# A feed-forward stage with split matmuls: one of its four input sums is made by GpSimd

## The reference

```python
h = rmsnorm(x, pre_ffn_norm[l])
f = (jax.nn.silu(h @ ffn_w_gate[l]) * (h @ ffn_w_up[l])) @ ffn_w_down[l]
x = x + rmsnorm(f, post_ffn_norm[l])
```

## Time and profile before

| | |
|---|---|
| median of 3 runs | 2581.53 us (2581.36 to 2581.83) |
| the profiled execution's own time | 2586.55 us |
| its span, first to last instruction | 2584.8 us |
| mean granted TensorE clock | 0.984 |
| TensorE busy | 2440.1 us (94%) |
| VectorE busy | 1441.7 us (56%) |
| ScalarE busy | 1065.3 us (41%) |
| GpSimd busy | 356.4 us (14%) |

### The profile page before, as it was taken

The page is one execution under the profiler, slowest core; times in us unless marked ns, Lnnn a source line. Parts: engine busy times, 40 slices in busy tenths (PEclk is TensorE's granted clock), DMA queues, the critical chain, the costliest instruction groups (busy, mean ns, idle before and its releaser), DMA issues. The chain is left out here.

```text
span 2584.8 us, 34173 instructions
## 1 busy us (share of the span) xinstructions
PE 2440.1 (94%) x12048; PEld 2028.8 (78%) x12048; DVE 1441.7 (56%) x1990; ACT 1065.3 (41%) x1877; POOL 356.4 (14%) x369
## 2 busy tenths in 40 slices
PE   7999999999899999999999898888899999999997
PEld 6788888877688888787878788887777788888886
DVE  3656566665423232364541477775468777776556
ACT  4767677776312121242222343432333323223444
POOL 0323333333000000000000235352000000000000
PEclk9999999999899999999999999999999999999999
DMA  3112111111212121332233210100333444337764
GB/s 129 34 33 67 34 59 41 50 33 33 87 46 80 48 81 49 114 106 72 89 113 115 90 50 25 49 24 0 122 111 122 171 159 170 139 142 251 246 187 171
DMA packets 98113, 241.74 MB, mean 94 GB/s; under 512 B 8800, under 2 KB 34784, under 8 KB 96608
## 3 DMA queue, kind: packets, MB, share of 16 engines
q1 hardware_dynamic: 98016, 240.50, 27.7%
HBM read 177.29 MB, written 63.18 MB: 93 GB/s over the span
## 5 line engine op out<-in xcount | busy, mean ns | idle before, releaser
L52 PE MATMUL psG<-h_hi,w_hi 128*128 128x512 f32 x1408 | 350.8, 399 | 15.0 <-ACT w_hi L77 6.5
L82 DVE TENSOR_TENSOR w_lo<-w_raw,w_hi 128x1024 fp32r<-128x1024 f32 x102 | 129.3, 1269 | 420.2 <-ACT w_hi L77 419.8
L52 PE MATMUL psG<-h_hi,w_lo 128*128 128x512 f32 x1408 | 339.8, 390 | 0.0
L52 PE MATMUL psG<-h_lo,w_hi 128*128 128x512 f32 x1408 | 339.6, 390 | 0.0
L52 PEld LDWEIGHTS psG<-h_hi,w_hi 128*128 128x128 f32 x1408 | 269.9, 193 | 73.9 <-issue 12.6
L52 PEld LDWEIGHTS psG<-h_lo,w_hi 128*128 128x128 f32 x1408 | 263.7, 188 | 54.8
L52 PEld LDWEIGHTS psG<-h_hi,w_lo 128*128 128x128 f32 x1408 | 263.5, 188 | 54.7
L77 ACT CAST w_hi<-w_raw 128x1024 fp32r<-128x1024 f32 x104 | 109.1, 1050 | 355.7 <-PE psG L52 317.2
L366 POOL TENSOR_TENSOR sb_later_lo<-sb_later,sb_later_hi 128x512 fp32r<-128x512 f32 (+3 forms) x80 | 90.6, 1133 | 173.7 <-ACT sb_later_hi L395 173.7
L1430 POOL MEMSET m_k_prev<- 128x128 f32 x1 | 0.2, 204 | 802.0 <-POOLq L1141 802.0
L530 DVE SCALAR_TENSOR_TENSOR sb_sp<-psA,sb_tmp 128x128 f32<-128x128 f32 (+2 forms) x96 | 53.5, 557 | 73.3 <-ACT sb_tmp L384 70.8
(11 more groups left out here) (471 smaller groups left out, 5243.2 us busy)
## 6 DMA issues: line engine op xcount, KB each, us to landing
w_raw<-in_units SPq DMA_DIRECT2D x140, 512.0 KB, 3.7
w_raw<-hidden_blocks SPq DMA_DIRECT2D x77, 256.0 KB, 2.9
features<-p_res SPq DMA_DIRECT2D x24, 512.0 KB, 2.8
w_spare<-in_units SPq DMA_DIRECT2D x22, 512.0 KB, 4.3
hidden_blocks<-features_T SPq DMA_DIRECT2D x11, 1024.0 KB, 3.9
down_sums<-w_spare SPq DMA_DIRECT2D x22, 512.0 KB, 3.4
ff_raw_up<-down_sums SPq DMA_DIRECT2D x44, 256.0 KB, 3.2
m_feat<-features SPq DMA_DIRECT2D x7, 1536.0 KB, 7.5
```

Of the source, the lines that this page charges most:

```text
L52: return pe.matmul(out, lhs, rhs, start=first, stop=last, skip_group_check=True)
L82: dve.tensor_tensor(self.lo[c % 2][:] if dest is None else dest, self.raw[c % 2][:], hi.bitcast(F32), ALU.subtract).then_inc(self.lo_done, 1)
```

## The change

The sum t2 is made by GpSimd's three instructions, in a program of its own for this block, in a tile `t3_raw` of 128x2048. That tile lies where t2's low part will be: `t_lo[:, 2]`, so `split_t(2)` writes its result over its own input. GpSimd's first sum waits for nothing, the others each for the one before, by the new semaphore `t3_made`; ScalarE's `turned(2)` waits for its third step. VectorE's three sums for t2 go. The other three sums stay with VectorE, t1 stays in `X2`, and the second sum for t3 gets a wait for the first. The values waited for on `turned_done` become smaller by what is gone (TensorE's 12 and 14 become 9 and 11, ScalarE's 11 becomes 9). To make room for the new semaphore, `spilled` and `stored` become one, `stored`, and the last wait of SyncE counts both kinds.

```diff
+            t3_raw = nc.alloc_sbuf_tensor_at("ff_t3_raw", [P, 4, HALF], F32, offset=nc.sbuf_base - 2 * 16 * HALF)
...
+        t_raw = [T_X[0], T_X[1], t3_raw[:], T_X[0]]
...
-                    sp.wait_ge(stored, 16 * NT)
+                    sp.wait_ge(stored, 32 * PAIRS + 16 * NT)
...
+            @block.gpsimd
+            def _(pool):
+                hq = lambda t, r, c: t[:, 4 * r:4 * r + 4, c * HALF:(c + 1) * HALF].bitcast(F32)
+                for n, (a, b, op) in enumerate(((hq(hT_hi, 1, 1), hq(hT_hi, 0, 1), ALU.subtract), (t3_raw[:], hq(hT_lo, 1, 1), ALU.add),
+                                                (t3_raw[:], hq(hT_lo, 0, 1), ALU.subtract))):
+                    if n:
+                        pool.wait_ge(t3_made, n)
+                    pool.tensor_tensor(t3_raw[:], a, b, op).then_inc(t3_made, 1)
...
                     elif q >= 3:
                         act.wait_ge(plain, 4)
-                        act.wait_ge(turned_done, 11)
+                        act.wait_ge(turned_done, 9)
...
                 def turned(n, need):
-                    act.wait_ge(turned_done, need)
-                    act.copy(t_hi[:, n], T_X[0 if n in (0, 3) else 1]).then_inc(t_hi_done, 1)
+                    act.wait_ge(t3_made if n == 2 else turned_done, need)
+                    act.copy(t_hi[:, n], t_raw[n]).then_inc(t_hi_done, 1)
...
-                    turned(2, 11)
+                    turned(2, 3)
...
                 def split_t(n):
                     dve.wait_ge(t_hi_done, n + 1)
-                    TT(t_lo[:, n], T_X[0 if n in (0, 3) else 1], t_hi[:, n].bitcast(F32), ALU.subtract).then_inc(turned_done, 1)
+                    TT(t_lo[:, n], t_raw[n], t_hi[:, n].bitcast(F32), ALU.subtract).then_inc(turned_done, 1)
...
                     TT(X1, hq(hT_hi, 1, 0), X2, ALU.subtract).then_inc(turned_done, 1)
-                    dve.wait_ge(turned_done, 8)
-                    TT(X2, hq(hT_hi, 1, 1), hq(hT_hi, 0, 1), ALU.subtract).then_inc(turned_done, 1)
+                    split_t(2)
                     dve.wait_ge(turned_done, 9)
-                    TT(X2, X2, hq(hT_lo, 1, 1), ALU.add).then_inc(turned_done, 1)
-                    dve.wait_ge(turned_done, 10)
-                    TT(X2, X2, hq(hT_lo, 0, 1), ALU.subtract).then_inc(turned_done, 1)
-                    split_t(2)
-                    dve.wait_ge(turned_done, 12)
                     for s in (sum3, sum1, sum2):
                         s(0, 1, 0)
```

More of the change, by code:

```diff
@@ L1986, in ring_raw @@
             return W.raw[r // 2][:, cols], raw_up[:, r // 2, cols]
-        plain, turned_done, t_hi_done = (sem(n) for n in ("plain", "turned_done", "t_hi_done"))
+        plain, turned_done, t_hi_done, t3_made = (sem(n) for n in ("plain", "turned_done", "t_hi_done", "t3_made"))
         raw_here = [sem(f"raw_here{s}") for s in range(2)]
@@ L1992, in layer2_ffn @@
         p1_done, evac, silu_done, mul = (sem(n) for n in ("p1_done", "evac", "silu_done", "mul"))
-        own_done, spilled, dw_sum, dw_stored = (sem(n) for n in ("own_done", "spilled", "dw_sum", "dw_stored"))
+        own_done, stored, dw_sum, dw_stored = (sem(n) for n in ("own_done", "stored", "dw_sum", "dw_stored"))
         r_here = [sem(f"r_here{s}") for s in range(R)]
@@ L1996, in layer2_ffn @@
         p1_b, evac_b = sem("p1_b"), sem("evac_b")
-        x_here, sq_a, sq_b, ms, rt, scaled, x_new, stored = (
-            sem(n) for n in ("x_here", "sq_a", "sq_b", "ms", "rt", "scaled", "x_new", "stored"))
+        x_here, sq_a, sq_b, ms, rt, scaled, x_new = (
+            sem(n) for n in ("x_here", "sq_a", "sq_b", "ms", "rt", "scaled", "x_new"))
         x_t = x_in.rearrange("(t p) d -> t p d", p=P)
@@ L2057, in spill @@
                     sp.wait_ge(own_done, 4 * n + 4 + 8 * i)
-                    sp.dma_start(a_dram[n + 2 * i][:, 0:4 * HALF], hid[n % 2].rearrange("p a t -> p (a t)")).then_inc(spilled, 16)
-                    sp.dma_start(a_dram[n + 2 * i][:, 4 * HALF:7 * HALF], own_all).then_inc(spilled, 16)
+                    sp.dma_start(a_dram[n + 2 * i][:, 0:4 * HALF], hid[n % 2].rearrange("p a t -> p (a t)")).then_inc(stored, 16)
+                    sp.dma_start(a_dram[n + 2 * i][:, 4 * HALF:7 * HALF], own_all).then_inc(stored, 16)
                 def start():
@@ L2090, in load_step @@
                     if p == 0 and j >= 8:
-                        sp.wait_ge(spilled, 32 * (j + 1))
+                        sp.wait_ge(stored, 32 * (j + 1))
                     if n == PAIRS:
@@ L2177, in first_half @@
                     first_copy(0, 1, 0)
-                    turned(3, 13)
+                    turned(3, 10)
                     high(4, 0, 1, 0)
@@ L2310, in c22 @@
                         if n > 1 or not isinstance(i, int):
-                            dve.wait_ge(spilled, 32 * (n - 1) + 64 * i)
+                            dve.wait_ge(stored, 32 * (n - 1) + 64 * i)
                         TT(quarter(hid[n % 2], 1, 1), banks[0][3], v, ALU.add).then_inc(evac, 1)
@@ L2346, in own_sum @@
                         if n or not isinstance(i, int):
-                            dve.wait_ge(spilled, 32 * n + 64 * i)
+                            dve.wait_ge(stored, 32 * n + 64 * i)
                         ins = TT(own[1], quarter(h, 0, 0), quarter(h, 0, 1), ALU.subtract)
@@ L2411, in first_half @@
                     hq = lambda t, r, c: t[:, 4 * r:4 * r + 4, c * HALF:(c + 1) * HALF].bitcast(F32)
+                    dve.wait_ge(turned_done, 8)
                     TT(T_X[0], T_X[0], hq(hT_lo, 1, 0), ALU.add).then_inc(turned_done, 1)
@@ L2418, in first_half @@
                     low(5, 0, 1, 0)
-                    dve.wait_ge(turned_done, 14)
+                    dve.wait_ge(turned_done, 11)
                     c22(0, 1, 0)
@@ L2513, in piece @@
                         if t == 0:
-                            dve.wait_ge(spilled, 32 * PAIRS)
+                            dve.wait_ge(stored, 32 * PAIRS)
                             dve.wait_ge(x_here, 16 * (NT + 1))
@@ L2614, in half_pair @@
                             pe.wait_ge(t_hi_done, {1: 2, 2: 3, 5: 4}[q])
-                            pe.wait_ge(turned_done, {1: 7, 2: 12, 5: 14}[q])
+                            pe.wait_ge(turned_done, {1: 7, 2: 9, 5: 11}[q])
                         pe.wait_ge(a_hi_done, count(7, kind, n, i, q + 1))
```

## The result

The changed kernel took 2593.6 us, the median of 7 executions (2588.11 to 2594.5), against 2581.83 (2581.35 to 2585.91) of 7 of the kernel before. The ratio of the two kernels is 1.0037, with a 95% interval of 1.0025 to 1.0048: slower. (It is not the ratio of the two medians, which is 1.0046; that of the two means is 1.0037 too.) The profiled execution took 2593.65, its span 2591.7. The forecast of 2588.5 said slower, by 0.27%, which lies in the interval; but the median lies above its range, which ended at 2590.5.

The account below looks back on a forecast made before the run. TensorE, busy 94% of the span, was taken as the bound. A 5.8 us wait plus 2.5 for the clock less a 1.35 gain gave + 6.95 on 2581.53, so 2588.5 us; range 2585.0 to 2590.5.

Parts of the forecast that it names:

- The slack of 7.1 us: Head of the feed-forward stage: VectorE makes w_lo of U0+2 7.1 us before TensorE needs it, so may be that late free.
- GpSimd's price: GpSimd's 128x2048 sums at the stage's head: 4.58 us each, 13.7 us for three, upper end 4.70 each.
- The turns: VectorE and GpSimd alternate strictly at the stage's head: 6.60 us a turn instead of 2.30, 12.9 us more for three.
- it makes no difference who goes first: Turns at the stage's head: all three fall ahead of w_lo of U0+2, whichever engine goes first.
- The clock: TensorE's clock falls to half behind the 5.8 us w_lo wait, costing 2.5 us; bounds 0 and 2.9.
- The gain: Three sums fewer on VectorE let c22 and what follows in the first pair come 1.35 us earlier; bounds 0 and 2.9.
- The sum for the stage: Wait for w_lo 5.8 plus clock 2.5 minus gain 1.35: + 6.95 us.

Follow-up runs that it names:

- one turn: Changed kernel with only the first of GpSimd's three sums, the others left out; executed once, stage 649.9 us against 651.2 before and 658.8 changed.
- two (8.8): Changed kernel with two of GpSimd's three sums, the last left out; executed once, stage 651.8 us against 651.2 before and 658.8 changed.
- GpSimd's memsets: Changed kernel with GpSimd's three sums replaced by three memsets of the same tile; executed once, stage 649.9 us.
- the copies: Changed kernel with GpSimd's three sums replaced by three copies of their first input to the same tile; executed once, stage 648.3 us.
- the fill run: Changed kernel with TensorE repeating 24 matmuls of unit U0+2 in the time of the w_lo wait; 2590.89 us, ratio 1.0022, stage 656.0 us.
- the 21 later executions: Changed kernel, unedited, run twice more beside the kernel before: 2593.35 us (10 executions, ratio 1.0033) and 2590.45 us (11, ratio 1.0024).
- the three intervals: 95% intervals of changed kernel against kernel before, first comparison and two unedited repeats: 1.0025 to 1.0048, 1.0023 to 1.0042, 1.0015 to 1.0033.

## Why the prediction was right in the stage and wrong in the time

**The slack of 7.1 us** at `w_lo` held: one turn (4.5 us) cost nothing, two (8.8) a wait of 1.59 us of idle time (1.8 by the starts), three (13.2) one of 5.93 (6.1 by the starts). Forecast for three: 12.9 us late and a wait of 5.8.

**GpSimd's price** was worked out as 4.58 us a sum from 0.40 and 2.35; measured 4.66 for the one that didn't wait.

**The turns** were forecast at 6.60 us for VectorE; they were 6.80 and 6.64 twice. That it makes no difference who goes first stays untested: in every run with sums GpSimd was first. That mattered for one thing: all three of VectorE's sums for t0 were held and not two, so `turned(0)`, forecast for about 1949, came at 1953.06 in a stage that started 0.7 us earlier. TensorE did not wait for it. Beside GpSimd's memsets, which only write, VectorE's first sum stayed at 2.29 us; beside instructions of GpSimd that read it took 6.80 (the sums) and 4.03 (the copies).

**The clock** was put at 2.5 us, the mean of what the earlier trace rows gives for the waits of 6.7 us (10 x 0.22 = 2.2) and 5.0 us (10 x 0.29 = 2.9); the granted clock behind each was 0.50 for its first 4 us, and 1.00 from 5 us (from 74.83) and from 6 us on (from 1074.62). Measured for the wait of 5.93: 2.9 in the windows, 2.8 by the starts and 2.8 by the fill run. A size, a little low.

**The gain** was put at 1.35 us: with one sum the stage gained 651.2 - 649.9 = 1.3. In the changed kernel 6.1 + 2.8 - 7.6 leaves 1.3, and `c22`, the step from which the forecast followed it, stands at 1987.56: 54.65 us after the stage's start in place of 47.03, 7.6 us later while TensorE is 8.9 late.

**The sum for the stage**, + 6.95, measured + 7.6. That the profile's span came out at 2591.7, against 2591.8 in the forecast, is luck: the stage was 0.65 us longer than forecast and happened to start 0.7 us earlier than in the profile before.

**The step that failed** is the last line of the sum: "that execution's own time was 2586.55, 1.75 outside the span and 5.0 above the median of the unprofiled runs, and the change leaves both distances as they are. Median: 2581.53 + 6.95". It took the 5.0 us for a fixed distance and 2581.53, with its 0.5 us between three executions, for the level of the kernel. Neither was so. Own time and span are 1.75 to 1.95 us apart in the profiles of both kernels, but the 5 us are the place of one execution in the spread of its kernel: they arise ahead of the stage, 3.0 us of the 5.5 between the two profiles at two falls of the clock in the first layer's mixers, which come in some executions and not in others. The three executions shown all lay at the lower end of a spread of 6 us with its mean at 2584.2. From there 7.5 us lead to 2591.7, the mean measured; the forecast's own 6.95 would have led to 2591.2, also above its range. The 2593.6 of the first seven is that plus chance: five of them lie above 2592, in the later group. The range was built of the stage's unknowns alone; it had no term for what lies ahead of the stage, and the profiled execution's 5 us were the sign of it. That the first seven arrived late by chance and not from the change is shown as far as the 21 later executions go, with a mean of 2591.5, and the three intervals, which all hold 1.0029.

## What to carry to other kernels

An elementwise instruction moved from VectorE to GpSimd need not free VectorE. Beside VectorE sums that read two tensors from SBUF, each sum moved saved 2.3 us here and cost 4.3 to 4.5, and the saving came late while the cost came at once. Before such a move, ask what VectorE will run in the same microseconds, and how much it may be late for its next customer. Beyond that slack TensorE waits, and the clock can add to it: 2.8 us on top of a wait of 5.9, 3.1 on top of 2.8, nothing on top of 1.6. And compare stages, from a fixed instruction to the end, rather than whole executions, when a change is worth less than their spread; three executions that agree don't show that spread, but a profile that disagrees with them does. A stage has its own chance too: with no fall of the clock at its head that of the copies was 1.6 us shorter than that of one sum.

## What of the hardware was not expected

- A GpSimd copy of 128x2048 from SBUF took 1.90 us, a memset 5.54 / 3 = 1.85, against 4.66 for a sum of two inputs. A copy makes VectorE's sum wait as a GpSimd sum does (4.03 us in place of 2.29), a memset doesn't (2.29).
- The granted clock falls at the same short waits of TensorE in some executions and not in others: at 575 to 600 and 630 to 645 us it was 0.93 and 0.89 or 1.00, and at the head of the feed-forward stage, behind the same wait of 2.63 us, 0.83 in 12 profiles and 1.00 in one. Each is worth 1.4 to 1.7 us. The two in the mixers are 3.0 of the 5.5 us between the two profiles of the kernel before.
